# A two-layer decoder trunk on one core: the middle projection by seven half products, and the last four weight sums by accumulating DMAs

## The chip, the core and the metric

The kernel is one program on one NeuronCore of a Trainium2 chip. TensorE (PE) multiplies, VectorE (DVE) and ScalarE (ACT) do elementwise work, GpSimd (POOL) does a little of it and issues software DMAs, SyncE (SP) issues most of the loads. The metric is the device time of one execution, in microseconds (us), lower is better.

## What is computed

Two layers on `x` of 512 tokens by 2048 features, all in float32:

```python
# layer 0
h = rmsnorm(x, e_norm_pre)
p = h @ e_w_in                      # 2048 x 7168, seven column groups
u = concat(ya * silu(a_z), yb * silu(b_z))   # gated convolutions, feature by feature
x = x + rmsnorm(u @ e_w_out, e_norm_post)    # the middle projection, 2048 x 2048
# layer 1
h = rmsnorm(x, o_norm_pre)
v, z = split(h @ o_w_in, 2)                  # 2048 x 4096
g = grouped_linear(pool_means(v) - v, o_c_w) + o_c_b
x = x + rmsnorm((g * o_c_scale * silu(z)) @ o_w_out, o_norm_post)  # the last projection
```

## The kernel before

**Products.** PE has no full float32 product at its full rate here: each operand is split into a rounded part (`w_hi`, `h_hi`, made by ACT) and the rest (`w_lo`, `h_lo`, made by DVE), and each product is three matmuls (lines 602, 604, 606), hi by hi, lo by hi, hi by lo. A matmul streams 512 columns (256 in a few stages). Weights come in slabs of 1 MB (128 partitions by 2048 elements) into `raw` or another buffer; ACT writes slot s mod 4 of `w_hi` once PE is done with slab s - 4 (`slab_done`), DVE then writes `w_lo` (`lo_ready`), and PE waits for `lo_ready`.

**Stages on PE, in order.** `h @ e_w_in` (56 slabs of 48 matmuls), the middle projection (16 slabs of 48, tokens on the output's partitions: `token_major` for three column blocks, `token_major_last` for the fourth, which finishes the tokens tile by tile), `h @ o_w_in` (32 slabs of 48; the first four slabs in two halves of 256 tokens each, h = 0 first), the grouped linear map (four groups of 48), and the last projection.

**The last projection** multiplies two matrices of 2 by 2 blocks (1024 by 1024 of the weights) with seven block products instead of eight. That takes 28 slabs of 24 matmuls. Slabs 0 to 3 are A11, 4 to 7 A12, 8 to 11 N1 and so on; slabs 24 to 27 are the last product, run in four parts: (tokens 0, column block 0), (0, 1), (1, 0), (1, 1), each 24 matmuls. Before the parts (0, 1) and (1, 1) PE waits for `c22(1)` on DVE (line 1638), since that reads the bank that they go on accumulating into; before (0, 0) and (1, 0) for `c22(0)`. Some products take combined weights: T1 (slabs 8 to 11), T2 (12, 13, 16, 17), T3 (20 to 23), T4 (24 to 27), each made from two pieces of 1 MB. Pieces live in the buffers c0 to c3 and b0 to b4. T1 and T3 are added by accumulating DMAs, SBUF to SBUF, issued by POOL (line 564); T2 and T4 by DVE (line 1609). T4's slab 24 is c0 += b1, 25 is c1 += b2, 26 is c2 += b3, 27 is c3 += b4, where b1 to b4 are loaded a fourth time, b1 after T3's last sum has landed (it was that sum's source), b4 after slab 22's low part.

**Norms between the layers.** In the middle, tokens are normed tile by tile (four tiles of 128) under the last column block: squares on ACT (`y_squares`), gain and residual on DVE (`y_gained`, `added`), squares again (`squares`), scaling (`scaled`), then 16 transposes on PE (line 635), rounding on ACT (`h_rounded`, line 915) and the rest on DVE (`h_rest`, line 1314). All these orders are written out by hand, engine by engine; an engine takes its instructions strictly in the order written, so a wait holds all that stands behind it.

## Time and profile before

| | us |
|---|---|
| median of 3 runs | 1384.14 (1383.84 to 1384.17) |
| the profiled execution's own time | 1384.06 |
| its span, first to last instruction | 1382.2 |
| PE busy | 1356.9, 98% of the span |
| DVE / ACT / POOL busy | 765.1 / 415.7 / 112.8 |
| middle projection on PE | 644.9 to 824.4 |
| last projection on PE | 1221.9 to 1374.4 |

"Busy" of PE is the union of its matmuls; the column "idle before" in the lists of groups tells what an engine waited for. A line number is one of the kernel before unless the text says otherwise. Times in windows and timelines count from the span's start.

### The profile page before, as it was taken

What the parts mean: (1) busy time and instruction counts of PE and PEld (TensorE: products, weight loads), DVE (VectorE), ACT (ScalarE), POOL (GpSimd) and SP (SyncE); (2) the same over time, 40 slices, a digit from 0 to 9 for tenths busy, and PEclk for the clock granted to TensorE, in tenths of its full rate; (3) what the DMA queues carried; (4) which work ended last, traced back from release to release, by engine and by line L of the source; (5) the groups of instructions that cost most, each with busy time, mean ns of one, the idle gap of its engine ahead of it and who ended that gap; (6) DMA issues with size and microseconds to landing.
All of it is one profiled execution on the core that took longest, in us unless ns stands there. A gap on an engine that the chain in (4) does not pass through costs nothing.

```text
span 1382.2 us, 15947 instructions
## 1 busy us (share of the span) xinstructions
PE 1356.9 (98%) x6370; PEld 1139.2 (82%) x6370; DVE 765.1 (55%) x784; ACT 415.7 (30%) x430; POOL 112.8 (8%) x109
## 2 busy tenths in 40 slices
PE   5999999999999999999999999999999999999997
PEld 4988888888888888888888889888888888878886
DVE  7588888888763322335322375544532222487778
ACT  5331233232222211224212243222222222345542
POOL 5100000000006400000000000000000001320000
PEclk9999999999999999999999999999999999999999
DMA  8233434343343333331622344433343333279666
GB/s 248 62 97 93 115 91 122 91 121 91 91 121 92 91 92 99 96 111 52 253 91 93 120 152 140 136 91 94 97 112 91 91 93 114 101 225 289 153 217 239
DMA packets 214119, 171.65 MB, mean 124 GB/s; under 512 B 2880, under 2 KB 187328, under 8 KB 211136
## 3 DMA queue, kind: packets, MB, share of 16 engines
q1 hardware_dynamic: 212064, 156.42, 37.1%
q0 software_dynamic: 1152, 8.39, 3.1%
q10 hardware_dynamic: 864, 6.29, 1.2%
q8 instruction: 28, 0.46, 0.1%
q14 instruction: 11, 0.09, 0.0%
HBM read 154.32 MB, written 8.39 MB: 118 GB/s over the span
## 4 chain that ended last, share of the span: by engine, by line
PE 97%; DVE 2%; DMA 0%; issue 0%; ACT 0%; SPq 0%; DVEq 0%; ACTq 0%
PE bank L602 32%; PE bank L604 32%; PE bank L606 32%; DVE h_lo L1349 1%; PE bank L635 1%; DMA rows<-x_t 0%; DVE rows L1342 0%; DVE scratch L1355 0%; DVE diagonals L1320 0%; DVE w_lo L1364 0%; DVE rows L1651 0%; PE bank L664 0%; PE bank L673 0%; ACT scratch L924 0%; SPq L321 0%
## 5 line engine op out<-in xcount | busy, mean ns | idle before, releaser
L602 PE MATMUL bank<-h_hi,w_hi 128*128 128x512 f32 (+1 forms) x1600 | 597.9, 374 | 5.1 <-DVE h_lo L1349 3.9
L604 PE MATMUL bank<-h_lo,w_hi 128*128 128x512 f32 (+1 forms) x1600 | 595.7, 372 | 0.0
L606 PE MATMUL bank<-h_hi,w_lo 128*128 128x512 f32 (+1 forms) x1600 | 595.7, 372 | 0.0
L602 PEld LDWEIGHTS bank<-h_hi,w_hi 128*128 128x128 f32 x1600 | 301.8, 189 | 59.6 <-issue 5.0
L604 PEld LDWEIGHTS bank<-h_lo,w_hi 128*128 128x128 f32 x1600 | 301.9, 189 | 52.8 <-issue 0.5
L606 PEld LDWEIGHTS bank<-h_hi,w_lo 128*128 128x128 f32 x1600 | 301.8, 189 | 52.3
L1287 DVE TENSOR_TENSOR w_lo<-raw,w_hi 128x2048 fp32r<-128x2048 f32 x105 | 243.6, 2320 | 123.7 <-ACT w_hi L892 108.9
L892 ACT ACTIVATE w_hi<-raw 128x2048 fp32r<-128x2048 f32 x106 | 202.7, 1912 | 152.7 <-PE bank L606 117.1
L1382 DVE SCALAR_TENSOR_TENSOR rows<-shifted,vecs,rows 128x512 f32 x256 | 198.0, 776 | 42.2 <-ACT rows L962 10.9
L602 PE MATMUL bank<-w_hi,h_hi 128*128 128x512 f32 x480 | 187.0, 390 | 0.0
L606 PE MATMUL bank<-w_hi,h_lo 128*128 128x512 f32 x480 | 186.8, 389 | 0.0
L604 PE MATMUL bank<-w_lo,h_hi 128*128 128x512 f32 x480 | 186.8, 389 | 0.0
L602 PEld LDWEIGHTS bank<-w_hi,h_hi 128*128 128x128 f32 x480 | 90.1, 188 | 19.1
L606 PEld LDWEIGHTS bank<-w_hi,h_lo 128*128 128x128 f32 x480 | 90.1, 188 | 18.9
L604 PEld LDWEIGHTS bank<-w_lo,h_hi 128*128 128x128 f32 x480 | 90.1, 188 | 18.2
L1548 DVE TENSOR_TENSOR shifted<-shifted 128x512 f32<-128x512 f32 x40 | 27.7, 693 | 84.7 <-ACT shifted L1082 83.9
L1567 DVE TENSOR_SCALAR scratch<-scratch,vecs x16 | 7.8, 488 | 109.9 <-ACT scratch L1103 109.9
L559 POOL TENSOR_TENSOR h_lo<-rows,h_hi 128x512 fp32r<-128x512 f32 x16 | 24.9, 1590 | 356.0 <-ACT h_hi L1091 356.0
L1103 ACT ACTIVATE scratch<-bank 128x512 f32 (+1 forms) x16 | 9.6, 598 | 133.0 <-PE bank L606 133.0
L980 ACT ACTIVATE scratch<-bank 128x512 f32<-128x512 f32 x16 | 9.6, 598 | 131.2 <-PE bank L606 131.2
L1082 ACT ACTIVATE shifted<-bank 128x512 f32<-128x512 f32 x16 | 9.6, 598 | 122.1 <-PE bank L606 122.1
L971 ACT ACTIVATE rows<-shifted,vecs 128x512 f32 x8 | 5.8, 724 | 125.0 <-DVE shifted L1407 125.0
(115 smaller groups left out, 629.5 us busy)
## 6 DMA issues: line engine op xcount, KB each, us to landing
raw<-e_in SPq DMA_DIRECT2D x54, 1024.0 KB, 5.6
raw<-o_in SPq DMA_DIRECT2D x32, 1024.0 KB, 6.2
raw<-e_out SPq DMA_DIRECT2D x16, 1024.0 KB, 5.0
spare<-o_out SPq DMA_DIRECT2D x12, 1024.0 KB, 8.9
scratch<-o_out SPq DMA_DIRECT2D x10, 1024.0 KB, 6.8
rows<-x_t SPq DMA_DIRECT2D x8, 512.0 KB, 6.6
x_mid<-rows ACTq DMA_DIRECT2D x4, 1024.0 KB, 4.8
raw<-o_cw SPq DMA_DIRECT2D x4, 1024.0 KB, 5.4
```

The costliest lines, as they stand in the source:

```text
L559: nc.gpsimd.tensor_tensor(h_lo[:, k, :], rows[:, k, :], f32(h_hi[:, k, :]), ALU.subtract).then_inc(pool_lo_ready, 1)
L602: nc.tensor.matmul(dst, w[0], m[0], start=first, stop=False, skip_group_check=goes_on)
L604: nc.tensor.matmul(dst, w[0], m[1], start=False, stop=False, skip_group_check=goes_on)
L606: return nc.tensor.matmul(dst, w[1], m[0], start=False, stop=last, skip_group_check=goes_on)
L635: last = nc.tensor.transpose(bank[4 + j][:, i * P:(i + 1) * P], row[:, k * P:(k + 1) * P], ident[:, :])
L892: nc.scalar.activation(w_hi[:, slot, :], raw[:, slot % RAW, :], ACT.Copy)\
L980: nc.scalar.activation(sz[buf], bank[q][:, :], ACT.Silu)\
L1082: nc.scalar.activation(v_row[:, PAD:], bank[q][:, :], ACT.Copy)\
L1287: nc.vector.tensor_tensor(w_lo[:, slot, :], raw[:, slot % RAW, :], f32(w_hi[:, slot, :]), ALU.subtract)\
L1349: nc.vector.tensor_tensor(h_lo[at], rows[at], f32(h_hi[at]), ALU.subtract)\
L1382: ins = nc.vector.scalar_tensor_tensor(out=dst, in0=row[:, at:at + T], scalar=tap(name, c, width, j), in1=dst, op0=ALU.mult, op1=ALU.add)
L1548: link(nc.vector.tensor_tensor(dst[:, PAD:], src[:, PAD:], src[:, PAD - step:PAD - step + T], ALU.add))
```

## The change

The middle projection now runs as the last one does: seven half products, 28 slabs of 24 matmuls (672 where 768 stood), with the same list of loads, sums, squares and block additions (`projection(0)`; the last is `projection(1)`). In both, T4 is no longer added by DVE but by four more accumulating DMAs (`t4_added`), so twelve of the sixteen weight sums are DMAs: four more in the last projection, twelve new ones in the middle.

The norm of the first two token tiles of the middle moves under that projection's last product (slabs 24 to 27): DVE takes mean squares, gains, `mid_added` (times the reciprocal root, plus the residual row; two instructions of 1024 columns) and `mid_scaled` (the second norm) between its low parts and `c22`. The post gain goes to buffer b1 once T4's first sum has landed; the residual rows of x to b0 and b4, the third and fourth to c3 and b0; SP issues these behind the fourth load of b4. PE transposes tile 0 after part (0, 1), tile 1 after part (1, 0), tile 2 after the first half slab of `h @ o_w_in` and tile 3 after the third. The high part of that stage's first slab (`split_ahead(AT_O1 - 1, 1)`) stands on ACT behind `mid_squares(2)`, its low part on DVE behind `mid_added(2)`.

`h` for `o_w_in` is stored with the two token halves apart, so a moving operand of 512 tokens is two runs of 256 (`both_halves`). In `rows` the blocks lie in chunks of 256, which makes several reads and writes on ACT, DVE and in stores three-dimensional. `group(g)` no longer waits for `pool_lo_ready`.

```diff
-E2 = NBLK
+E2 = 7
...
-SLOT_A, SLOT_B, SLOT_C, SLOT_D = range(4)
+SLOT_AT = ({"A": 2, "B": 1, "C": 3, "D": 0}, {"A": 0, "B": 1, "C": 2, "D": 3})
...
-        ADDED_AT = {n: i + 1 for i, n in enumerate((12, 13, 16, 17, 24, 25, 26, 27))}
+        FIRST = (AT_E2 * SLOTS, AT_O2 * SLOTS)
+        LOADS = {name: (1 if name[0] == "c" else 4) for name in buffers[0]}
+        ADDED_AT = {n: i + 1 for i, n in enumerate((12, 13, 16, 17))}
...
+            def sums_loads(layer, w):
+
+                low_done(layer, 4)
...
+                sp.wait_ge(t3_added[3], 16 * (layer + 1))
+                low_done(layer, 19)
+                piece(layer, w, "b1", 1, 0, 0, 0)
+                low_done(layer, 20)
+                piece(layer, w, "b2", 1, 0, 0, 1)
+                low_done(layer, 21)
+                piece(layer, w, "b3", 1, 0, 1, 0)
+                low_done(layer, 22)
+                piece(layer, w, "b4", 1, 0, 1, 1)
+
...
+            sums_loads(0, e_out)
+            sp.wait_ge(t4_added[0], 16)
+            sp.dma_start(gain_post[0], e_post.to_broadcast([P, D])).then_inc(gain_loaded, 16)
+            low_done(0, 23)
+            sp.dma_start(x_resid[0], x[0:P, :]).then_inc(resid_loaded[0], 16)
+            sp.wait_ge(t4_added[3], 16)
+            sp.dma_start(x_resid[1], x[P:2 * P, :]).then_inc(resid_loaded[1], 16)
+            low_done(0, 26)
+            sp.dma_start(gain_next, o_pre.to_broadcast([P, D])).then_inc(gain_next_loaded, 16)
+            low_done(0, 27)
+            sp.dma_start(x_resid[2], x[2 * P:3 * P, :]).then_inc(resid_loaded[2], 16)
             with sp.Fori(0, O1V + O1Z) as g:
...
+            sums_loads(1, o_out)
+            low_done(1, 24)
+            sp.dma_start(gain_post[1], o_post.to_broadcast([P, D])).then_inc(gain_loaded, 16)
...
+            def add_by_dma(layer, dst, src, dst_loads, src_loads, news):
+
+                for name, count in ((dst, dst_loads), (src, src_loads)):
+                    pool.wait_ge(piece_loaded[name], 16 * (count + layer * LOADS[name]))
+                nc.gpsimd.dma_start(buffers[layer][dst], buffers[layer][src],
+                                    accum_op=ALU.add).then_inc(news, 16)
...
+                add_by_dma(layer, "b0", "b1", 4, 3, t3_added[3])
+                pool.wait_ge(lo_ready, first + 13)
+                add_by_dma(layer, "c0", "b1", 1, 4, t4_added[0])
+                pool.wait_ge(lo_ready, first + 14)
+                add_by_dma(layer, "c1", "b2", 1, 4, t4_added[1])
+                pool.wait_ge(lo_ready, first + 17)
+                add_by_dma(layer, "c2", "b3", 1, 4, t4_added[2])
+                pool.wait_ge(lo_ready, first + 18)
+                add_by_dma(layer, "c3", "b4", 1, 4, t4_added[3])
+
+            weight_sums(0)
             powers(MID, 2 * TT)
+            pool.wait_ge(normed, 2 * TT)
+            nc.gpsimd.memset(shifted[:, :, 0:PAD], 0.0).then_inc(pads_set, 1)
 
...
+            def both_halves(k):
+                return h_halves[0][:, :, k, :], h_halves[1][:, :, k, :]
...
+                        between(tt, nb)
+
+            def first_transposes(tt, nb):
+                if (tt, nb) == (0, 1):
+                    transposes(0, x_resid[0])
+                elif (tt, nb) == (1, 0):
+                    transposes(1, x_resid[1])
...
+            def o_half_slab(q, h):
...
+                    m = h_halves[0][:, h, k, :], h_halves[1][:, h, k, :]
+                    last = product(bank[q][:, h * HALF:(h + 1) * HALF], weights(q, k, P), m,
+                                   k == 0, k == KT - 1)
...
+            projection(0, AT_E2 + 1, lambda b: uses4(b, "mid") + 1, first_transposes)
...
+                    o_half_slab(q, h)
+                    if h == 0 and q in (0, 2):
+                        transposes(2 + q // 2, x_resid[2 + q // 2])
...
+            high_dma(0, 25, t4_added[1])
+            high_dma(0, 26, t4_added[2])
+            c_squares(0, C22, 0, c22_ready, 8)
+            high_dma(0, 27, t4_added[3])
+            mid_squares(0)
+            c_squares(0, C22, 1, c22_ready, 10)
+            mid_squares(1)
+            h_rounded(0)
+            last_squares(0, 0)
+            h_rounded(1)
+            act.dma_start(x_resid[3], x[3 * P:4 * P, :]).then_inc(resid_loaded[3], 16)
+            mid_squares(2)
+            split_ahead(AT_O1 - 1, 1, STEPS)
+            last_squares(0, 1)
+            split_ahead(AT_O1 - 1, 2, STEPS)
+            mid_squares(3)
+            h_rounded(2)
+            split_ahead(AT_O1 - 1, 3, STEPS)
+            split_ahead(AT_O1, 0, STEPS)
+            h_rounded(3)
 
...
+            dve.wait_ge(c_squared, 8)
+            mean_square(MID)
+            dve.wait_ge(gain_loaded, 16)
+            gain(0, c_half(C11, 0), c_half(C11, 0), 0, 8)
+            gain(0, c_half(C12, 0), c_half(C12, 0), NH, 8)
+            low(0, 25)
+            c22(0, 0)
+            dve.wait_ge(c_gained, 2)
+            mid_added(0)
+            low(0, 26)
+            mean_square(MID + 2)
+            gain(0, c_half(C11, 1), c_half(C11, 1), 0, 8)
+            gain(0, c_half(C12, 1), c_half(C12, 1), NH, 8)
+            low(0, 27)
+            c22(0, 1)
...
+            mid_mean(0)
+            dve.wait_ge(c_gained, 4)
+            mid_added(1)
+            mid_scaled(0)
+            for tt in range(2):
+                gain(0, c_half(C22, tt), c_half(C22, tt), NH, 12)
+            mid_mean(1)
+            mid_scaled(1)
             h_rest(0)
-            mid_norm(2)
+            dve.wait_ge(c_squared, 14)
+            mean_square(MID + 4)
+            last_gain(0, 0, 0)
+            last_gain(0, 1, 0)
+            for nb in range(2):
+                dve.wait_ge(bank_free[2 * nb], AT_O1 + 1)
+            dve.wait_ge(c_gained, 6)
             h_rest(1)
-            split_ahead(end, 1)
-
-            def under_last_norm():
-                h_rest(2)
-                split_ahead(end, 2)
-
-            mid_norm(3, under_last_norm, lambda: split_ahead(end, 3))
-            split_ahead(end + 1, 0)
+            mid_added(2)
+            split_ahead(AT_O1 - 1, 1)
+            mid_mean(2)
+            last_gain(0, 0, 1)
+            dve.wait_ge(c_squared, 16)
+            mean_square(MID + 6)
+            last_gain(0, 1, 1)
+            for nb in range(2):
+                dve.wait_ge(bank_free[2 * nb + 1], AT_O1 + 1)
+            mid_scaled(2)
+            mid_added(3)
+            split_ahead(AT_O1 - 1, 2)
+            h_rest(2)
+            mid_mean(3)
+            split_ahead(AT_O1 - 1, 3)
+            mid_scaled(3)
+            split_ahead(AT_O1, 0)
             h_rest(3)
...
+            projection(1)
+            low(1, 25)
+            c22(1, 0)
+            low(1, 26)
+            dve.wait_ge(c_squared, 16 + 8)```

POOL's DMAs of the last projection, kernel before, from T1's last sum on (`spare2`, `spare3`, `spare4` are b2, b3, b4; `raw` is c0 and c1; `scratch` the others):

```order
L564 DMA scratch_55<-spare2_70 128x2048
L564 DMA spare2_70<-spare3_71 128x2048
L564 DMA spare3_71<-spare4_72 128x2048
L564 DMA spare4_72<-scratch_55 128x2048
L564 DMA scratch_55<-scratch_55 128x2048
L530 TENSOR_TENSOR rstd_67<-meansq_66,minus_half_62 128x1 x4
```

The same place in the kernel after:

```order
L582 DMA spare4_74<-scratch_55 128x2048
L582 DMA scratch_55<-scratch_55 128x2048
L582 DMA raw_52<-scratch_55 128x2048
L582 DMA raw_52<-spare2_1_71 128x2048
L582 DMA scratch_55<-spare3_1_73 128x2048
L582 DMA scratch_55<-spare4_74 128x2048
L553 TENSOR_TENSOR rstd_67<-meansq_66,minus_half_62 128x1 x4
```

Four DMAs, the sums for slabs 24 to 27, now stand behind the four of T3 in POOL's queue.

DVE at the end of the last projection, kernel before (L1609 is a sum, L1601 a low part, L1638 `c22`):

```order
L1609 TENSOR_TENSOR raw_52<-raw_52,spare2_70 128x2048
L1601 TENSOR_TENSOR w_lo_54<-raw_52,w_hi_53 128x2048
L1609 TENSOR_TENSOR scratch_55<-scratch_55,spare3_71 128x2048
L1601 TENSOR_TENSOR w_lo_54<-raw_52,w_hi_53 128x2048
L1638 TENSOR_TENSOR rows_51<-rows_51,bank0 128x512
L1638 TENSOR_TENSOR rows_51<-rows_51,bank1 128x512
L1609 TENSOR_TENSOR scratch_55<-scratch_55,spare4_72 128x2048
L1601 TENSOR_TENSOR w_lo_54<-scratch_55,w_hi_53 128x2048
```

DVE at the end of the middle projection, kernel after (L1454 is a low part, L1521 a gain, L1513 `c22`, L1592 `mid_added`):

```order
L1454 TENSOR_TENSOR w_lo_54<-raw_52,w_hi_53 128x2048
L1291 TENSOR_REDUCE total_65<-sumsq_64 128x1
L1292 TENSOR_SCALAR meansq_66<-total_65 128x1
L1521 TENSOR_TENSOR rows_51<-rows_51,scratch_55 128x4x256 x2
L1454 TENSOR_TENSOR w_lo_54<-raw_52,w_hi_53 128x2048
L1513 TENSOR_TENSOR rows_51<-rows_51,bank0 128x2x256
L1513 TENSOR_TENSOR rows_51<-rows_51,bank1 128x2x256
L1592 SCALAR_TENSOR_TENSOR rows_51<-rows_51,rstd_67,scratch_55 128x4x256 x2
L1454 TENSOR_TENSOR w_lo_54<-scratch_55,w_hi_53 128x2048
```

Where sums stood, the norm of the first tokens stands, ahead of the low parts of slabs 25, 26 and 27.

ACT in the middle, kernel after, from the rounding of tile 1 (L920) to the high part of the first slab of `o_w_in` (L907); L1171 is `mid_squares`, L1190 the load of the fourth residual row:

```order
L920 ACTIVATE h_hi_49<-bank7 128x4x128
L1190 DMA scratch_55<-x 128x2048
L1171 ACTIVATE junk_63,sumsq_64<-rows_51 128x512 x2
L1176 DMA x_mid<-rows_51 128x4x256
L1171 ACTIVATE junk_63,sumsq_64<-rows_51 128x512 x2
L1176 DMA x_mid<-rows_51 128x4x256
L907 ACTIVATE w_hi_53<-raw_52 128x2048
```

In the kernel before, that high part stood here, ahead of the squares of a third tile:

```order
L915 ACTIVATE h_hi_49<-bank7 128x4x128
L1056 DMA scratch_55<-x 128x2048
L892 ACTIVATE w_hi_53<-raw_52 128x2048
L1028 ACTIVATE shifted_56,sumsq_64<-bank3 128x512
L915 ACTIVATE h_hi_49<-bank4 128x4x128
```

The squares of tile 2 (four instructions) moved ahead of the high part.

## Rows read from the trace of the kernel before

**Rows 1.** The page: the span, shares of the engines, the chain that ended last.

```profile
span 1382.2 us, 15947 instructions
...
PE 1356.9 (98%) x6370; PEld 1139.2 (82%) x6370; DVE 765.1 (55%) x784; ACT 415.7 (30%) x430; POOL 112.8 (8%) x109
...
PE 97%; DVE 2%; DMA 0%; issue 0%; ACT 0%; SPq 0%; DVEq 0%; ACTq 0%
```

**Rows 2.** PE in stretches: from:to, length, busy time (matmuls), clock, DMA share, GB/s.

```profile
80.00:420.00 340.00, 340.00 (x1501) 1.00 0.37 102
...
670.00:790.00 120.00, 120.00 (x531) 1.00 0.31 106
...
1215.00:1370.00 155.00, 155.00 (x686) 1.00 0.75 231
```

**Rows 3.** DVE's timeline, end of the last projection: start, duration, instruction, [idle before].

```profile
1330.59 2.29 DVE L1609 TENSOR_TENSOR raw<-raw,scratch 128x2048 f32<-128x2048 f32 x1 [0.85 <-DMA scratch<-o_out]
...
1354.65 2.29 DVE L1601 TENSOR_TENSOR w_lo<-scratch,w_hi 128x2048 fp32r<-128x2048 f32 x1 [2.48 <-ACT w_hi L1128]
1356.86 1.28 DVE L1638 TENSOR_TENSOR rows<-rows,bank 128x512 f32<-128x512 f32 x2
```

**Rows 4.** ACT's timeline, same place: slab 27's high part, and the last square.

```profile
1352.70 1.92 ACT L1128 ACTIVATE w_hi<-scratch 128x2048 fp32r<-128x2048 f32 x1 [2.30 <-PE bank L606]
...
1374.40 0.60 ACT L1162 ACTIVATE junk<-bank 128x512 bf16<-128x512 f32 x1 [4.75 <-PE bank L606]
```

**Rows 5.** SP's timeline: the fourth loads of b1, then of b2, b3, b4.

```profile
1325.50 0.37 SPq L394 DMA_DIRECT2D scratch<-o_out  x1
1325.92 4.22 SPq L394 DMA_DIRECT2D spare<-o_out  x3
```

**Rows 6.** DMA queues in 1328:1337, loads alone: packets, MB, share of 16 engines.

```profile
q1 hardware_dynamic: 1780, 3.55, 105.2%
```

**Rows 7.** The same view in 1320:1324, one accumulating DMA alone.

```profile
q0 software_dynamic: 107, 0.88, 108.0%
```

**Rows 8.** The same view in 1257:1266, accumulating DMAs (q0) and loads (q1) together.

```profile
q0 software_dynamic: 219, 1.66, 88.7%
q1 hardware_dynamic: 218, 0.45, 14.7%
```

**Rows 9.** Issue to landing: the accumulating DMAs of line 564, then `spare`'s in 1240:1350.

```profile
DMA to landing us min/median/max: 7.0/7.7/14.9
...
DMA to landing us min/median/max: 5.0/8.0/21.6
```

**Rows 10.** Groups with shapes, 1205:1382: count, busy us, mean ns, idle before.

```profile
L1162 ACT ACTIVATE junk<-rows 128x512 bf16<-128x512 f32 x12 | 7.4, 615 | 3.0 <-DVE rows L1638 3.0
L1644 DVE TENSOR_TENSOR rows<-rows,raw 128x1024 f32<-128x1024 f32 x6 | 7.1, 1220 | 0.0
...
L1651 DVE SCALAR_TENSOR_TENSOR rows<-rows,rstd,scratch 128x1024 f32<-128x1024 f32 x4 | 5.0, 1282 | 0.1
```

**Rows 11.** DVE's and ACT's timelines in the middle: rest, rounding and first high part.

```profile
819.28 2.47 DVE L1314 TENSOR_TENSOR h_lo<-bank,h_hi 128x512 fp32r<-128x512 f32 x4
821.67 2.28 DVE L1287 TENSOR_TENSOR w_lo<-raw,w_hi 128x2048 fp32r<-128x2048 f32 x1
...
815.49 2.04 ACT L915 ACTIVATE h_hi<-bank 128x512 fp32r<-128x512 f32 x4
817.39 1.94 ACT L892 ACTIVATE w_hi<-raw 128x2048 fp32r<-128x2048 f32 x1
```

**Rows 12.** PE's timeline after its start: 256-column matmuls, two early, two later.

```profile
22.60 0.41 PE L606 MATMUL bank<-h_hi,w_lo 128*128 128x256 f32 x1
22.81 0.41 PE L602 MATMUL bank<-h_hi,w_hi 128*128 128x256 f32 x1
...
25.28 0.28 PE L602 MATMUL bank<-h_hi,w_hi 128*128 128x256 f32 x1
25.40 0.28 PE L604 MATMUL bank<-h_lo,w_hi 128*128 128x256 f32 x1
```

More of the change, by code:

```diff
@@ new lines, in _, with mid_added @@
+            low(0, 3)
+            a_low(0, "B", 0, quarter(A12), FORMS[0]["a12"][0])
+            projection(0)
+            def mid_added(t):
+                n = MID + 2 * t
+                dve.wait_ge(rstd_ready, NORM_ORDER.index(n) + 1)
+                dve.wait_ge(resid_loaded[t], 16)
+                for m, c in enumerate((C11, C12) if t < 2 else (C21, C22)):
+                    at = c_half(c, t % 2)
+                    nc.vector.scalar_tensor_tensor(
+                        out=at, in0=at, scalar=rstd[:, n:n + 1],
+                        in1=chunks(x_resid[t][:, m * NH:(m + 1) * NH]),
+                        op0=ALU.mult, op1=ALU.add).then_inc(x_mid_ready, 1)
```

1116 lines of the change are left out of this document (505 added, 611 removed).

## The prediction

> **What bounds the kernel.** I read the page first, then PE by stretches, then the other engines and the DMA queues where the change works. The page says that PE is busy for 98% of the span and that the chain that ended last runs 97% on PE [rows 1]. The stretches say that this is no average over mixed stages: in long windows of `h @ e_w_in`, of the middle projection and of the last one PE is busy all the time, with a matmul of 512 columns each 0.2265, 0.2260 and 0.2260 us (340 / 1501, 120 / 531, 155 / 686) [rows 2]. So each matmul taken away is worth 0.2265 us, as long as nothing else comes late, and each microsecond that another engine or a DMA comes late is paid in full. The question is thus what is ready only just in time.
>
> I call E the start of slab 24 in the last projection. PE is done at 1374.4 [rows 4], the last product is 96 matmuls or 21.8 us, so E is 1352.6; ACT's high part of slab 27, which waits for slab 23 alone, starts at 1352.70 and confirms it [rows 4]. A part takes 24 x 0.2265 = 5.4 us, so part (0, 1) wants the first `c22(1)` at E + 5.4 = 1358.1. DVE's low part of slab 27 starts at 1354.65 and `c22(1)` behind it at 1356.86, its first half done some 0.7 later [rows 3]: 1357.5, half a microsecond before PE wants it. This place has no slack.
>
> **Removed.** The middle projection falls from 768 to 672 matmuls: 96 x 0.2265 = 21.7 us less. The 64 transposes stay. The products lie on the path now, so this is a gain in full.
>
> **T4 by DMA in the last projection.** Off DVE go four sums of 2.3 us, but the one for slab 24 already waited 0.85 us for its piece b1 [rows 3], so the pieces come just in time now; what is new comes on top. The loads: b1 is issued at 1325.50, b2 to b4 up to 1330.1 [rows 5]. What does a transfer cost? Loads alone move 3.55 MB in 9 us with all 16 engines busy [rows 6], so a piece of 1.05 MB takes 2.66 us of all engines; one alone lands 5.0 us after its issue [rows 9], 2.3 more than it moves. An accumulating DMA alone moves 0.88 MB in 4 us with the engines likewise busy [rows 7], 4.8 us each; it lands after 7.0 at best [rows 9], 2.2 more. Nothing overlaps, the engines being full, so the last sum lands no sooner than 1325.5 + 2.3 + 4 x 2.66 + 4 x 4.8 = 1357.6. Both kinds together: q0 takes 88.7% of the engines' time and the loads 14.7% [rows 8]. So the load of b4, in the ring behind b2 and b3, is starved while the first three sums move (loads in that stage took up to 21.6 us [rows 9]); the fourth sum, which needs b4, starts only then, and its own 2.2 us come on top: 1359.8. The gain row and a residual row of 1 MB each share the engines with it, up to 2 x 2.66; I take 4 of those 5.3 and have 1363.8, E + 11.2.
>
> From there the high part takes 1.9 [rows 4], the low part 2.3 and half of `c22(1)` 0.7 [rows 3]: 1368.7, where PE wants it at 1358.1. **10.5 us** of PE standing still. The bounds: with the fourth sum at 1357.6, 4.3 us; with 14.9 us for it (the longest [rows 9]) from a landing of b4 at 1352, 13.6.
>
> **The same in the middle.** The list of slabs, loads and sums is the same and DVE is not behind there, so the last sum lands at about E0 + 9 to E0 + 11 (E0, its slab 24). By that alone the wait is 8 to 10 us. But a second chain runs on DVE. The gain e_post may be loaded only into b1, once the first sum has landed (about E0 - 12: 1325.5 + 5.0 for b1, then 10 to 12 for a sum among loads), and stands in SP's ring behind the starved b4: I take it to land at E0 + 3. The first gain stands ahead of the low part of slab 25 on DVE, and all that follows is queued: gains 2 x 1.2, low part 2.2, `c22(0)` 1.2, `mid_added` 2 x 1.25, low part 2.2, mean square 0.3, gains 2.4, low part 2.2, half of `c22(1)` 0.6 [rows 3, 10]: 16.0. So `c22(1)` is ready at E0 + 19 where PE wants it at E0 + 5.4: 13.6; I take **12**, since b1's chain may be some 2 us ahead here. Lower bound 4 (no gain row late, last sum as early as above), upper 15.
>
> **The norm at the start of `h @ o_w_in`.** Let Z be the end of tile 1's transposes. PE has 5.4 us of part (1, 1) left. Meanwhile, each waiting for the one before: rounding of tile 1, of which the first quarter is 0.6 [rows 11], `h_rest(1)` 2.5 [rows 11], `mid_added(2)` 2.5 [rows 10], the second pair of squares 1.3 [rows 10], the high part of the first slab 1.9 and its low part 2.3 [rows 11]. That is 11.1, so PE stands for 5.7. Then DVE has mean squares and gains (1.8), `mid_scaled(2)` and `mid_added(3)` (2 x 2.5) and the second slab's low part 2.2: Z + 20, where PE, with the half slab (5.4) and tile 2's transposes (1.7), is at Z + 18.3. Together **7.4**. In the kernel before that high part stood ahead of the squares and was done at 819.3 where PE wanted it at 824.4 [rows 11].
>
> **TensorE's clock.** PE waits long in three or four places then. Just after its idle start the 256-column matmuls come 0.21 us apart, the lower level of 1.2 GHz; later 0.12, the upper of 2.4 [rows 12]. About ten matmuls at 0.09 us more are 1 us. I add **2** for the ramps that are not under another wait (0 to 4). The Trainium skill, "TensorE: Matmul & The Clock Gate", Part 1, says that the clock falls back on idleness, so it speaks for a ramp after each long wait; this trace has no long gap behind its start to show it. [...]
>
> **At nothing.** Reads in chunks of 256 on ACT and DVE: `h_rest` writes such chunks and takes 0.62 each [rows 11], like a contiguous block. The start of the middle projection: the form of A11 is made from the second quarter of the last slab of `e_w_in` on, some 3 us ahead of PE. A moving operand in two runs: taken at nothing, since no row has one. Its bound is that each run costs like an instruction of its own: 0.12 us for 256 columns [rows 12] twice is 0.24 against 0.2265, times 28 x 48 matmuls, 18 us. One square at a time on ACT: under 1 us, under PE's products. The Trainium skill, "DMA: Bandwidth & Descriptors", Queues, rings and completion order, has each engine take a packet from each ring in turn; if that gave the loads half of the time, b4 and the gain would be there some 10 us sooner, and the middle's term would be near 9 instead of 12. The split of 88.7 to 14.7 [rows 8] says otherwise.
>
> **The sum.** 1384.1 - 21.7 + 10.5 + 12 + 7.4 + 2 = **1394.3**, against the profiled execution's own 1384.06, which is within 0.1 of the median, so I forecast 1394.
>
> **The rivals.**
> - Faster (1): the sums come in time, as T1's and T3's do now, and DVE, rid of four sums, is early. Speaks for it: no row of before shows PE waiting for a DMA. Against: T3's sums come one by one between loads, and T4's four come within 25 us. Then only the 7.4 remains: 1369.7. It decides at the landing of the last sum: before E + 1 all is hidden.
> - In between (2): both projections at their lower bounds, 4.3 and 4, or halfway to mine: 1378 to 1387.
> - Slower still (3): two runs cost, up to 18 more; or each wait brings a full ramp. 1397 to 1412.
> - That the products are not fewer can be excluded: the order shows 28 slabs of 24 in the middle.
>
> **How the numbers follow.** Mine 0.60 (1388 to 1401), (1) 0.15, (2) 0.15, of it a third below 1381.3, half within 0.2% of before and a sixth above that, (3) 0.10. A measurement can tell about 0.2%, 2.8 us. Faster 0.15 + 0.05 = 0.20, same 0.08, slower 0.72. The range leaves out (1) and the far part of (3): 1379 to 1402.
>
> **What would show it.** In the profile after: the middle projection has 672 matmuls; PE idle some 10 us before part (0, 1) in the last projection, released by DVE `c22(1)`, with ACT's high part of slab 27 released by a DMA; in the middle the same with DVE waiting for the gain row, and a wait of 6 us before the first half slab of `h @ o_w_in`. If high part 27 in both is released by PE, the step on the DMAs is wrong. If matmuls of `o_w_in` come further apart than 0.2265, two runs cost.

## The result: slower by 1.2%

| kernel | median us | runs | lowest to highest |
|---|---|---|---|
| before | 1383.99 | 4 | 1383.78 to 1384.17 |
| after | 1399.97 | 4 | 1398.93 to 1403.02 |

The ratio is 1.012, 95% interval 1.0106 to 1.0133. The forecast was 1394 with a range of 1379 to 1402 and 0.72 for slower. The profiled execution took 1398.93 us, the shortest of its four, 14.9 more than that of before (1384.06).

### The profile page after: what moved, and what is told of

It reads as the page before. It is cut to its first block, busy times and chain, and to the rows that moved or that the text cites. A ratio compares the mean times of both kernels' runs of the same rounds, so it can differ in the third digit from the quotient of the medians.

```text
span 1397.1 us, 15727 instructions
## 1 busy us (share of the span) xinstructions
PE 1342.1 (96%) x6274; PEld 1125.4 (81%) x6274; DVE 810.0 (58%) x781; ACT 450.7 (32%) x445; POOL 128.0 (9%) x126
## 4 chain that ended last, share of the span: by engine, by line
PE 90%; DMA 5%; DVE 4%; ACT 1%; issue 1%; DVEq 0%; ACTq 0%; POOLq 0%
PE bank L630 30%; PE bank L632 30%; PE bank L634 30%; DMA spare<-o_out 2%; DMA scratch<-e_post 1%; DMA raw<-scratch 1%; DMA scratch<-spare 1%; DVE h_lo L1336 1%; DVE w_lo L1454 1%; DVE scratch L1342 1%; ACT w_hi L1013 0%; PE bank L666 0%; DVE rows L1329 0%; DMA rows<-x_t 0%; DVE rows L1592 0%
## 5 line engine op out<-in xcount | busy, mean ns | idle before, releaser
L630 PE MATMUL bank<-h_hi,w_hi 128*128 128x512 f32 (+1 forms) x1600 | 598.5, 374 | 10.7 <-DVE w_lo L1281 4.9
L632 PE MATMUL bank<-h_lo,w_hi 128*128 128x512 f32 (+1 forms) x1600 | 596.2, 373 | 0.0
L634 PE MATMUL bank<-h_hi,w_lo 128*128 128x512 f32 (+1 forms) x1600 | 596.1, 373 | 0.0
L630 PEld LDWEIGHTS bank<-h_hi,w_hi 128*128 128x128 f32 x1600 | 302.3, 189 | 65.9 <-issue 5.7
L632 PEld LDWEIGHTS bank<-h_lo,w_hi 128*128 128x128 f32 x1600 | 302.3, 189 | 52.6 <-issue 0.5
L634 PEld LDWEIGHTS bank<-h_hi,w_lo 128*128 128x128 f32 x1600 | 302.3, 189 | 52.3
L1281 DVE TENSOR_TENSOR w_lo<-raw,w_hi 128x2048 fp32r<-128x2048 f32 x89 | 207.1, 2327 | 53.5 <-ACT w_hi L907 46.6
L630 PE MATMUL bank<-w_hi,h_hi 128*128 128x512 f32 x448 | 177.2, 395 | 24.1 <-DVE rows L1513 24.0
L907 ACT ACTIVATE w_hi<-raw 128x2048 fp32r<-128x2048 f32 x90 | 171.9, 1910 | 77.6 <-PE bank L634 64.9
L632 PE MATMUL bank<-w_lo,h_hi 128*128 128x512 f32 x448 | 176.0, 393 | 0.0
L634 PE MATMUL bank<-w_hi,h_lo 128*128 128x512 f32 x448 | 175.8, 392 | 0.0
L630 PEld LDWEIGHTS bank<-w_hi,h_hi 128*128 128x128 f32 x448 | 85.2, 190 | 43.4 <-DVE rows L1513 25.8
L634 PEld LDWEIGHTS bank<-w_hi,h_lo 128*128 128x128 f32 x448 | 85.2, 190 | 18.1
L632 PEld LDWEIGHTS bank<-w_lo,h_hi 128*128 128x128 f32 x448 | 85.4, 191 | 17.6
L1454 DVE TENSOR_TENSOR w_lo<-scratch,w_hi 128x2048 fp32r<-128x2048 f32 x26 | 59.9, 2303 | 52.7 <-ACT w_hi L1013 52.7
L1013 ACT ACTIVATE w_hi<-scratch 128x2048 fp32r<-128x2048 f32 x26 | 49.8, 1916 | 70.2 <-DMA scratch<-spare 22.7
L1454 DVE TENSOR_TENSOR w_lo<-raw,w_hi 128x2048 fp32r<-128x2048 f32 x16 | 37.4, 2336 | 41.4 <-ACT w_hi L1013 41.4
```

The lines of the kernel that those rows point to most:

```text
L630: nc.tensor.matmul(dst, w[0], m[0], start=first, stop=False, skip_group_check=goes_on)
L632: nc.tensor.matmul(dst, w[0], m[1], start=False, stop=False, skip_group_check=goes_on)
L634: return nc.tensor.matmul(dst, w[1], m[0], start=False, stop=last, skip_group_check=goes_on)
L907: nc.scalar.activation(w_hi[:, slot, :], raw[:, slot % RAW, :], ACT.Copy)\
L1013: nc.scalar.activation(w_hi[:, s % SLOTS, :], buffers[layer][SPLIT_FROM[s]], ACT.Copy).then_inc(hi_ready, 1)
L1281: nc.vector.tensor_tensor(w_lo[:, slot, :], raw[:, slot % RAW, :], f32(w_hi[:, slot, :]), ALU.subtract)\
```

## The profile after

The page says where to look: PE has fewer matmuls (6274 for 6370, [rows 1]) and is busy for 96% of a longer span. The chain that ended last, 97% on PE before, has 9% on DMAs and DVE. The last row is the group of the high by high matmuls in the two projections; what stands behind the bar is the idle time before them.

```profile
span 1397.1 us, 15727 instructions
...
PE 1342.1 (96%) x6274; PEld 1125.4 (81%) x6274; DVE 810.0 (58%) x781; ACT 450.7 (32%) x445; POOL 128.0 (9%) x126
...
PE 90%; DMA 5%; DVE 4%; ACT 1%; issue 1%; DVEq 0%; ACTq 0%; POOLq 0%
...
L630 PE MATMUL bank<-w_hi,h_hi 128*128 128x512 f32 x448 | 177.2, 395 | 24.1 <-DVE rows L1513 24.0
```

Line 1513 is `c22`. The timeline of PE at the waits (start, duration, instruction, idle before): three are released by `c22`, one by a low part.

```profile
775.09 0.39 PE L634 MATMUL bank<-w_hi,h_lo 128*128 128x512 f32 x1
783.92 0.80 PE L630 MATMUL bank<-w_hi,h_hi 128*128 128x512 f32 x1 [8.44 <-DVE rows L1513]
...
790.82 0.39 PE L634 MATMUL bank<-w_hi,h_lo 128*128 128x512 f32 x1
794.44 0.79 PE L630 MATMUL bank<-w_hi,h_hi 128*128 128x512 f32 x1 [3.23 <-DVE rows L1513]
...
815.65 0.39 PE L634 MATMUL bank<-w_hi,h_lo 128*128 128x512 f32 x1
820.98 0.58 PE L630 MATMUL bank<-h_hi,w_hi 128*128 128x256 f32 x1 [4.93 <-DVE w_lo L1281]
...
1358.13 0.39 PE L634 MATMUL bank<-w_hi,h_lo 128*128 128x512 f32 x1
1370.86 0.79 PE L630 MATMUL bank<-w_hi,h_hi 128*128 128x512 f32 x1 [12.35 <-DVE rows L1513]
1371.45 0.63 PE L632 MATMUL bank<-w_lo,h_hi 128*128 128x512 f32 x1
...
1374.41 0.39 PE L634 MATMUL bank<-w_hi,h_lo 128*128 128x512 f32 x1
```

The last four show both parts of a loss. From the end of the matmul at 1358.13 (0.23 later by the spacing) to 1370.86 PE stands for 12.5 us. Then eight matmuls take 3.55 us (1374.41 - 1370.86) where eight take 1.81 at 0.2265: 1.7 us at TensorE's lower level, 0.427 us for 512 columns. I call this a ramp.

By PE's timeline the middle, from its first product to the end of tile 3's transposes, took 198.5 us before (644.94 to 843.46) and 198.7 after (644.76 to 843.43). The last projection, first to last matmul, took 152.1 before (1221.88 to 1373.97) and 166.8 after (1221.89 to 1388.71). So **the middle lost just what its 96 matmuls gave, and the last projection lost 14.7 us with nothing in return.**

Why was `c22` late? The chain of waits for the last projection, followed back from its end (start, duration, what):

```profile
1329.78 24.80 DMA spare<-o_out
1354.65 0.60 issue
1355.25 10.70 DMA scratch<-spare
1365.97 1.92 ACT w_hi L1013
1368.16 1.96 issue
1370.12 0.69 DVE rows L1513
```

The load of b4 took 24.8 us from issue to landing, the fourth sum behind it 10.7 more, then come high part, low part (the second "issue" covers it) and `c22(1)`. While b4 was under way the engines worked almost wholly for the sums (queues in 1336:1341, as in [rows 8]: packets, MB, share of 16 engines):

```profile
q0 software_dynamic: 117, 0.96, 91.9%
q1 hardware_dynamic: 115, 0.24, 14.0%
```

The same for the middle's wait before part (0, 1). This chain does not go through the last sum, but through the gain row and DVE's queue behind it: 753.08 is T4's first sum, whose landing lets the gain row be loaded.

```profile
753.08 11.59 DMA raw<-scratch
764.70 13.99 DMA scratch<-e_post
779.85 1.22 DVE rows L1521
784.47 2.39 DVE rows L1592 x2
786.86 2.20 DVE w_lo L1454
791.59 2.20 DVE w_lo L1454
793.79 0.61 DVE rows L1513
```

And a stretch of `h @ o_w_in`, for the moving operand in two runs (the columns of [rows 2]). In the same stretch of before PE has the same 1325 matmul records in 300 us.

```profile
900.00:1200.00 300.00, 300.00 (x1325) 248.43 (x1324) 103.01 (x109) 72.86 (x67) 14.97 (x11) 1.00 0.35 102
```

## The experiments

**First group: who adds T4.** `BY_DVE` lists, for each layer, the slabs whose sum DVE makes; `add_t4` adds on DVE if the slab is in it and does nothing otherwise, POOL leaves these out, and `high_t4` waits on ACT for the one or the other. The edit (here the last projection; from kernel to kernel the list differs, and where DVE makes sums of the middle too, `add_t4(0, 27)` stands ahead of `mid_added(0)`):

```diff
+        BY_DVE = ((), (24, 25, 26, 27))
...
-                high_dma(layer, 24, t4_added[0])
+                high_t4(layer, 24)
...
                 low(layer, 22)
+                add_t4(layer, 24)
                 low(layer, 23)
                 c12(layer, 1)
+                add_t4(layer, 25)
                 low(layer, 24)
+                add_t4(layer, 26)
...
             c22(1, 0)
+            add_t4(1, 27)
```

*The last projection by DVE (e1_last_dve).*

> The changed kernel, but T4's four weight sums of the last projection are added by DVE again, at the places they had in the kernel before; the middle is as changed. Theory (the accumulating DMAs of the last projection cost what its trace shows: 12.5 us of PE standing before part (0, 1), 1.7 us of matmuls at the lower clock behind that wait, 0.4 us at the start of slab 24, 14.7 together against before): the wait goes altogether, 1399.97 - 14.7 = 1385.3 us, and the last projection takes 152.1 us as in the kernel before. Rival (the chunked reads and the third dimension slow DVE and ACT, so that DVE can't carry its four sums in time any more): 2 to 5 us of wait remain, 1387 to 1390. Rival (the DMA sums only moved a wait that is there anyway): no change, 1400.

Measured 1385.14 us (1384.13 to 1385.80, ratio to before 0.9998 to 1.0017): the theory's figure. The last projection takes 152.1 us again, and no wait of it is left; b4, issued at 1329.9, lands after 11.8 us, not 24.8 (the view of its line):

```profile
DMA to landing us min/median/max: 11.8/11.8/11.8
```

This rules out both rivals: chunked reads don't keep DVE from its sums, and the wait isn't there without the DMA sums.

*The middle by DVE (e2_mid_dve).*

> The changed kernel, but T4's four sums of the middle projection are added by DVE, at the same places as in the last projection of the kernel before; the gain row is loaded once DVE has added slab 24's sum. The last projection is as changed. In the changed kernel PE stood for 8.6 and 3.4 us in the middle and paid 1.6 us of slow clock behind each, 15.2 us. Theory (DVE is then the bound, since two pairs of gains, mid_added and a mean square, 7.5 us, stand ahead of c22(1), which came 0.5 us early without them): a wait of about 7.0 us and one ramp of 1.7 remain, 1399.97 - 15.2 + 8.7 = 1393.5 us. Rival (the late DMAs alone were the cause): all 15.2 us go, 1384.8. Rival (DVE's order was the cause, and four more sums of 2.3 us make it worse): 1400 or more.

Measured 1391.19 us (1390.81 to 1392.41). The middle took 188.3 us in place of 198.7, so 10.4 less, where I had expected 6.5: the wait before (0, 0) went, the one before (0, 1) fell to 3.2 us and not to 7.0. DVE is the bound, as the theory says, but it had more room ahead of the last product than I gave it.

```profile
784.26 0.80 PE L645 MATMUL bank<-w_hi,h_hi 128*128 128x512 f32 x1 [3.04 <-DVE rows L1541]
```

The time fell by less than 10.4 since this execution's last projection, which is the changed one, took 169.1 us, not 166.8: in the four kernels that leave it as changed (after, this one, e5_mid_order and e6_o_order) it took 166.8 to 169.1 us. The 2.3 us more here are a wait before part (0, 1) that ended 1.3 us later, counted from the projection's first matmul, and a ramp behind it that cost 2.8 us in place of 1.7.

*Both by DVE (e3_both_dve).*

> The changed kernel with T4's sums by DVE in both projections. Theory: the two savings add up, -14.7 and -6.5, 1378.8 us, which would be 5 us faster than the kernel before. If the waits were one common cost (the queues of both projections held by the same thing) they would not add up.

Measured 1374.42 us (1374.26 to 1376.11), ratio to before 0.9933, interval 0.9917 to 0.9950: **faster than both kernels.** The two savings of the trace, 10.4 and 14.7, add up: 1398.9 - 25.1 = 1373.8 against a profiled execution of 1374.38.

*Only the fourth sum by DVE (e4_one_dve).*

> The changed kernel, but in the last projection the fourth sum of T4 alone (slab 27, from b4) is added by DVE; the first three stay DMAs. Theory (the load of b4, starved beside three sums, lands at 1354.6 as it did, and only the fourth sum behind it goes, 11 us of DMA for 2.3 us of DVE): c22(1) half done at 1362.4 where it was at 1370.8, so PE still stands for about 4 us and pays its ramp; 1391.6 us. Rival (the cost is the engine time of the sums, a quarter each): -3.7 us, 1396.3. Rival (everything hangs on the last sum alone, and b4 comes in time without it): -14.7, 1385.3.

Measured 1394.13 us (1392.71 to 1395.61): 5.8 less by the medians, between the theory (8.4 less) and a quarter each (3.7 less). By the trace the last projection took 162.2 us for 166.8, 4.6 less, which is nearer to the quarter. b4 took 26.5 us to land, as starved as before, but the chain of waits now goes through the third sum, which landed at 1358.3, so that slab 26 was late as well:

```profile
1346.30 11.98 DMA scratch<-spare
```

And b4's load, from the view of its line:

```profile
DMA to landing us min/median/max: 26.5/26.5/26.5
```

So the fourth sum alone is not the cause. It is the row of them, with loads beside them that get about a seventh of the engines.

*The first two by DMA, the last two by DVE, in both projections (e8_split).*

> The changed kernel with T4's first two sums (slabs 24, 25) by DMA and its last two (26, 27) by DVE, in both projections. With all four by DVE the middle still had a wait of 3.2 us and its ramp of 1.6 before part (0, 1), DVE being the bound. Theory (the first two sums land at 764.7 and 770.3, ahead of need, and take 4.6 us off DVE; b4 is starved only until the second has landed, some 3 us ahead of the last product): that wait goes too, 1374.4 - 4.8 = 1369.6 us. Rival (two sums among the loads already make b3, b4 or the gain row late): 1376 to 1386.

Measured 1389.88 us (1388.99 to 1390.09): the rival. In the last projection two sums still cost 5.4 us (157.5 for 152.1). In the middle the gain row is late again, since it waits for the first sum and shares the engines with the second; it lands at 774.3 where with four sums by DVE it landed at 764.0. DVE then works without a pause for 18 us until `c22(1)`, and the middle takes 198.5 us, as if nothing had been undone.

```profile
774.34 2.36 DVE L1549 TENSOR_TENSOR rows<-rows,scratch 128x1024 f32<-128x1024 f32 x2 [3.41 <-DMA scratch<-e_post]
...
791.53 1.28 DVE L1541 TENSOR_TENSOR rows<-rows,bank 128x512 f32<-128x512 f32 x2
```

*T4 by DMA alone, in the kernel before (f1_before_t4).*

```diff
+            for n, (s, dst, src) in enumerate(((13, "c0", "b1"), (14, "c1", "b2"),
+                                               (17, "c2", "b3"), (18, "c3", "b4"))):
+                pool.wait_ge(lo_ready, LAST + s)
...
+                add_by_dma(dst, src, t4_added[n])
...
-            add(24, 4)
```

> The kernel before with one part of the change alone: T4's four sums in the last projection by accumulating DMAs in place of DVE. Theory (this part costs by itself what the changed kernel lost there, 12.5 us of wait, 1.7 of slow clock behind it and 0.4 at the start of slab 24): 1384.0 + 14.7 = 1398.7 us. Rival (the loss needs something else of the change, the chunked layout or the state the middle leaves the queues in): 1384 to 1390.

Measured 1399.81 us (1399.26 to 1400.50), 15.6 more than before beside it (1384.26), where I had expected 14.7; by its trace the last projection took 167.2 us for 152.1, 15.1 more. The same part costs about the same in a kernel that has nothing else of the change:

```profile
1371.09 0.79 PE L610 MATMUL bank<-w_hi,h_hi 128*128 128x512 f32 x1 [11.31 <-DVE rows L1651]
```

**Second group: which chain binds the middle (e5_mid_order).** DVE takes two low parts and `c22(0)` ahead of the gains:

```diff
+            low(0, 25)
+            c22(0, 0)
+            low(0, 26)
             dve.wait_ge(gain_loaded, 16)
             gain(0, c_half(C11, 0), c_half(C11, 0), 0, 8)
             gain(0, c_half(C12, 0), c_half(C12, 0), NH, 8)
-            low(0, 25)
-            c22(0, 0)
             dve.wait_ge(c_gained, 2)
             mid_added(0)
-            low(0, 26)
```

> The changed kernel, but in the middle DVE takes the low parts of slabs 25 and 26 and c22(0) ahead of the first two gains (and so ahead of the wait for the gain row). T4's sums stay DMAs. Theory (two chains end at c22(1): DVE's queue from the gain row's landing at 778.7 on, and the last sum's landing at 785.98; with the queue eased the last sum is next): high part, low part and half of c22(1) behind 785.98 give 790.8 where part (0, 1) began at 794.4, so 3.6 us less, and one wait of 10 us in place of two, so one ramp of 1.6 less: 1394.8 us. Rival (the gain row alone made the middle late): 15.2 us go, 1384.8. Rival (the last sum alone set it, DVE's order is nothing): no change but the place of the wait, 1398 to 1400.

Measured 1399.14 us (1398.00 to 1400.06). The time alone can't be told from the changed kernel's and lies where the second rival put it, 1398 to 1400. The trace decides: the mechanism is right and the sum is not. Part (0, 1) began at 791.26 (790.8 expected), 3.2 sooner, and the last sum is what binds now:

```profile
786.37 1.91 ACT L1013 ACTIVATE w_hi<-scratch 128x2048 fp32r<-128x2048 f32 x1 [6.77 <-DMA scratch<-spare]
...
791.26 0.79 PE L630 MATMUL bank<-w_hi,h_hi 128*128 128x512 f32 x1 [10.16 <-DVE rows L1513]
```

But I had counted the first wait's ramp as a gain of its own. It had lain inside the time until 794.4 already, since `c22(1)` ends at its own time whatever PE does. And the one ramp left was longer, 12 matmuls at 0.427 in place of 6 or 7, 2.7 us in place of 1.5. The middle gave 1.6 us, not 5.2.

**The order at the start of `h @ o_w_in` (e6_o_order).**

```diff
-            mid_squares(2)
             split_ahead(AT_O1 - 1, 1, STEPS)
+            mid_squares(2)
...
-            mid_added(2)
             split_ahead(AT_O1 - 1, 1)
+            mid_added(2)
```

> The changed kernel, but the first slab of h @ o_w_in is split ahead of tile 2's norm: on ACT its high part stands before mid_squares(2), on DVE its low part before mid_added(2). Theory (the 5.1 us and the ramp of 1.7 before the first half slab come from this order alone): they go, and tile 2's own chain, 2.2 us later on DVE, makes PE wait some 1.3 us before tile 2's transposes: 1394.5 us. Rival (the wait only moves to tile 2's transposes, since the whole chain of the norm is the bound): 1398 or more. Rival (nothing behind it is late): 1393.2.

Measured 1401.99 us (1401.27 to 1403.78): my theory fell, the first rival held. The stage began without a wait, 6.7 us sooner (5.1 are the wait; the rest is that the wait before (0, 1), 2.1 us this time, had no ramp behind it), and PE waited behind it, for tile 2's transposes and again before the second half slab, with a ramp of 2.8 us there; tile 3's transposes came 0.6 us later than in the changed kernel. (The rest of the difference is this execution's last projection, 168.4 us.)

```profile
822.44 2.70 PE L666 MATMUL bank<-ident,scratch 128*128 128x128 f32 x16 [1.99 <-DVE scratch L1603]
828.23 0.58 PE L630 MATMUL bank<-h_hi,w_hi 128*128 128x256 f32 x1 [3.09 <-DVE w_lo L1281]
```

**What a ramp costs (e7_warm).** Ahead of three waits, matmuls of no use:

```diff
+            WARM = {(0, 0, 0): 34, (0, 0, 1): 12, (1, 0, 1): 50}
...
+                        stay_warm(layer, WARM.get((layer, tt, nb), 0))
                         pe.wait_ge(c22_ready, at + 2 * nb + tt + 1)
```

> The changed kernel with matmuls that compute nothing wanted (into bank 4, free at that time, 512 columns each) put on PE ahead of the waits of the last product: 34 and 12 in the middle, before parts (0, 0) and (0, 1), and 50 in the last projection before part (0, 1); at 0.2265 us they fill 7.7 of 8.6, 2.7 of 3.4 and 11.3 of 12.5 us of waiting. Theory (the seven matmuls at 0.427 us behind each wait are the lower clock, which comes from the idleness, and cost 1.5 to 1.7 us each): they go, 1399.97 - 4.9 = 1395.1 us, and the matmuls behind the waits come 0.2265 apart at once. Rival (those seven are slow for another reason, such as fresh weights or DMA traffic): no change, 1400.

Measured 1397.95 us (1397.11 to 1399.45). All three ramps are gone (the second matmul behind each wait starts 0.33 or 0.34 us after the first and the rest come 0.23 apart, where it was 0.59 and 0.43), so it is the idle time that brings them:

```profile
784.64 0.50 PE L630 MATMUL bank<-w_hi,h_hi 128*128 128x512 f32 x1 [1.22 <-DVE rows L1523]
784.97 0.39 PE L632 MATMUL bank<-w_lo,h_hi 128*128 128x512 f32 x1
...
795.15 0.50 PE L630 MATMUL bank<-w_hi,h_hi 128*128 128x512 f32 x1 [2.06 <-DVE rows L1523]
...
1370.93 0.50 PE L630 MATMUL bank<-w_hi,h_hi 128*128 128x512 f32 x1
1371.26 0.40 PE L632 MATMUL bank<-w_lo,h_hi 128*128 128x512 f32 x1
```

But the time fell by 2.0 us (1.6 between the profiled executions), not 4.9: the middle took 198.6 us, as in the changed kernel. A ramp ahead of another wait is free, because that wait ends when DVE ends. Only the last projection's, with nothing but products behind it, gave its 1.7 (165.1 us for 166.8).

**Third group: on from T4 by DVE in both.** In f2_best DVE takes tile 1's mean square and gains behind `c22(1)`:

```diff
             low(0, 26)
-            mean_square(MID + 2)
-            gain(0, c_half(C11, 1), c_half(C11, 1), 0, 8)
-            gain(0, c_half(C12, 1), c_half(C12, 1), NH, 8)
             low(0, 27)
             c22(0, 1)
+            mean_square(MID + 2)
+            gain(0, c_half(C11, 1), c_half(C11, 1), 0, 8)
+            gain(0, c_half(C12, 1), c_half(C12, 1), NH, 8)
             mid_mean(0)
+            mid_scaled(0)
             dve.wait_ge(c_gained, 4)
             mid_added(1)
-            mid_scaled(0)
```

> T4 by DVE in both projections (1374.42 us), and in the middle DVE takes the mean square and the two gains of tile 1 behind c22(1), and mid_scaled(0) ahead of mid_added(1). With T4 by DVE the middle's part (0, 1) began at 784.8 where PE wanted it at 781.5, DVE having worked without a pause since 759. Theory (DVE's queue is the bound of that wait, 2.7 us of it are moved behind): c22(1) half done at 782, the wait and its ramp go; tile 0's transposes then wait for mid_scaled(0), which waits for the gain row o_pre (landed 787.0): first half at 788.2, 3.3 us sooner than 791.8: 1371.1 us. Rival (the time is set by tile 1's norm, later now by mid_scaled(0) ahead of it): 1374 or more. Rival (everything behind comes in time): 1369.5.

Measured 1375.59 us (1373.78 to 1376.09), the first rival, and not to be told from the 1374.42 of e3_both_dve (1374.26 to 1376.11). The wait before (0, 1) fell to 0.5 us and had no ramp, tile 0's transposes start at 787.3, and tile 1's wait: DVE scales tile 1 at 793.71, and with T4 by DVE and the old order it did so at 793.57. DVE has the same work in any order. PE is released a little later by DVE's `h_rest(0)` (line 1324), which must free the bank and stands behind that:

```profile
793.71 2.48 DVE L1634 SCALAR_TENSOR_TENSOR spare<-rows,rstd,scratch 128x1024 f32<-128x1024 f32 x2 [0.66 <-POOL rstd L564]
...
796.94 1.30 PE L681 MATMUL bank<-ident,spare 128*128 128x128 f32 x5 [2.19 <-DVE h_lo L1324]
```

Then f3_best, the same with 20 matmuls of no use before `h @ o_w_in`, and one swap on DVE:

```diff
-            mid_added(3)
             split_ahead(AT_O1 - 1, 2)
+            mid_added(3)
```

> As f2_best, and before h @ o_w_in 20 matmuls that compute nothing wanted (4.5 us of the 5.1 that PE waits there), and DVE splits the second slab of that stage ahead of mid_added(3). The first half slab ran at 0.213 us for 256 columns for its first 17 matmuls, 1.7 us more than at 0.117. Theory (the ramp goes; the second slab's low part, now at 2.4 us less, is ready as PE asks for it; tile 3's scaling, 2.3 us later, is about in time): 1.5 us less than f2_best. Rival (as in the middle of e7_warm, where two of three ramps removed moved nothing because the next wait ends at a fixed time): the same as f2_best within 0.5 us.

Measured 1378.64 us (1377.96 to 1380.14): neither. Both edits are in this one kernel, so only the trace tells them apart. The ramp, 2.7 us in f2_best, went (tile 2's transposes came at 816.6, not 819.6), but the swap I had added to make use of it cost more. `mid_added(3)` later means that ACT's squares of tile 3, and behind them its rounding of tile 2, are later; DVE waits 2.4 us for that, and PE for the low part behind:

```profile
821.98 2.48 DVE L1333 TENSOR_TENSOR h_lo<-bank,h_hi 128x512 fp32r<-128x512 f32 x4 [2.40 <-ACT h_hi L944]
...
827.59 0.58 PE L645 MATMUL bank<-h_hi,w_hi 128*128 128x256 f32 x1 [3.37 <-DVE w_lo L1313]
```

Last, g1_pool_gains: T4 by DVE in both, and four gains on POOL:

```diff
+            powers(MID, 1)
+            pool.wait_ge(gain_loaded, 16)
+            pool_gain(c_half(C11, 1), 0, 8)
+            pool_gain(c_half(C12, 1), NH, 8)
+            powers(MID + 1, 2)
+            for tt in range(2):
+                pool_gain(c_half(C22, tt), NH, 12)
...
-            for tt in range(2):
-                gain(0, c_half(C22, tt), c_half(C22, tt), NH, 12)
```

> T4 by DVE in both projections (1374.42 us), and in the middle the two gains of tile 1 and the two of C22 are taken by POOL, which is idle there, in place of DVE: 4.7 us less for DVE, about 12 us (four blocks of 1024 at 3.04 us, from its 1.52 us for 128x512) for POOL. In f2_best the order on DVE was changed and tile 1's scaled row was done at 796.1 as before. Theory (DVE's whole queue from 759 to 796 is the bound of the middle now, whatever its order): c22(1) comes 2.3 us sooner, tile 1's scaling some 4.7 sooner, and PE, which then waits at tile 0's transposes for the gain row o_pre (787.0, first half scaled 788.2), begins tile 1's at 795.5 instead of 799.0: 1374.4 - 3.4 = 1371.0 us. Rival (POOL and DVE slow each other when both work, or POOL's powers come late behind its gains): 1374 or more.

Measured 1379.35 us (1378.44 to 1380.15), the rival. DVE's groups with shapes in the stretch 786:796 (count, busy us, mean ns), first of e3_both_dve, then of this kernel with POOL's in 766:796.

```profile
L1623 DVE SCALAR_TENSOR_TENSOR rows<-rows,rstd,spare 128x1024 f32<-128x1024 f32 x2 | 2.5, 1282 | 0.0
```

```profile
L1637 DVE SCALAR_TENSOR_TENSOR rows<-rows,rstd,spare 128x1024 f32<-128x1024 f32 x2 | 4.6, 2349 | 0.3 <-issue 0.3
L1648 DVE SCALAR_TENSOR_TENSOR scratch<-rows,rstd,scratch 128x1024 f32<-128x1024 f32 x2 | 4.6, 2334 | 0.0
...
L629 POOL TENSOR_TENSOR rows<-rows,scratch 128x1024 f32<-128x1024 f32 x4 | 13.8, 3460 | 0.2 <-ACT junk L1106 0.2
```

DVE's 1.28 us became 2.3 beside POOL's work, and POOL's gains took 3.46, where I had estimated 3.04 from twice its 1.52 for 128x512. What DVE was rid of (4.7 us) it more than paid back: these two pairs took 9.2 us for 5.0, and a low part and T4's last sum beside the other gains 7.8 for 4.6, about 7.5 us more in all. That agrees with the Trainium skill, "SBUF — State Buffer", Who interferes with whom, which says that a DVE instruction with two SBUF inputs contends with a GpSimd instruction that reads SBUF.

## Why the prediction held, point by point

The forecast was 6 us too low. Its mechanisms held: the starved load and the late last sum, DVE's queue behind the gain row, and the norm's chain before `h @ o_w_in`. Its sizes did not: three costs were too low by 2.4, 1.7 and 3.0 us and one too high by 2.3, so that a part of the error cancelled by luck. What the changes cost was forecast as 31.9 us (10.5 + 12 + 7.4 + 2); measured it is 14.9 + 21.7 = 36.6, and the other 1 us is the median above the profiled execution.

| term | forecast | measured in the trace of after |
|---|---|---|
| 96 matmuls fewer | -21.7 | -21.7 |
| last projection, T4 by DMA | 10.5 | 12.5, and 0.4 at slab 24's start |
| middle, until part (0, 1) | 12 | 13.7 |
| start of `h @ o_w_in` | 7.4 | 5.1 |
| ramps not under another wait | 2 | 1.5 + 1.8 + 1.7 = 5.0 |

- **The last projection: right in kind, 2 us short.** b4 landed at 1354.65 and the fourth sum at 1365.95, where I had 1363.8. The sum itself took 10.7 us, 3.7 more than the 7.0 of one alone, which is about the 4 that I allowed for loads beside it. What came late is its start: 1355.25, where my sum implies 1352.8 (1359.8 less 7.0). I had counted the gain row and one residual row, both beside the last sum. There were two residual rows, and in 1325.5:1354.65, before b4 had landed, the loads moved 4.87 MB, 0.7 more than the four pieces. In 1354.65:1366, beside the sum, they moved 2.47 MB more (the view of the queues):

```profile
q1 hardware_dynamic: 348, 2.47, 51.8%
```

That makes 3.1 MB of rows, three and not two. No run holds these rows back, so what they cost by themselves is not shown. e1_last_dve and f1_before_t4 price this part at 14.8 and 15.6, ramp included, and the landing times of b4, 11.8 against 24.8, show the starved load.
- **The middle: the chain held to 0.1 us, the discount did not.** The gain row landed at 778.69, 3.4 after E0 = 775.3 (forecast 3); part (0, 1) began at E0 + 19.1 (forecast 19). The chain gave 13.7; I took 12, "since b1's chain may be some 2 us ahead", and it was not. The place was partly wrong: I had all of the wait before part (0, 1), but 8.6 of it stood before (0, 0), since the low part of slab 25 stands behind the gains. e5_mid_order shows that two chains end there 3 us apart, and that the gain row's is the longer.
- **The start of `h @ o_w_in`: 5.1 for the 5.7 forecast, and the second wait of 1.7 did not come.** The first half slab took 7.5 us (820.98 to 828.51): 48 matmuls at 0.12 are 5.8, where I had written 5.4, and the ramp's 1.8 came on top, so the second slab's low part, done at 829.8, was ready when tile 2's transposes were through. e6_o_order shows how close it is: with the first wait taken away, the second appears.
- **The clock: the term that was mis-sized, by 3 us.** I took 2 of a possible 4 from ten matmuls; four ramps came, each 1.5 to 1.8, one of them hidden. The three others came to 5.0 us, above the 4 that I had as the most: no row of before has a ramp behind a wait, and the runs price one at 1.4 to 3.0 us. The Trainium skill, "TensorE: Matmul & The Clock Gate", Part 1, says that the clock falls back on idleness; the traces agree, since e7_warm, which fills the idle time, has none of the three ramps.
- **At nothing:** two runs of 256 columns cost nothing (1325 matmul records in 300 us before and after), which takes rival (3)'s first half away; its second half, a full ramp for each wait, is what happened. 1399.97 lies in that rival's span (1397 to 1412) and in my own case's (1388 to 1401). The chunked reads cost nothing that e1_last_dve could show: its last projection took the 152.1 us of before.
- **The queue rule.** I set the share of [rows 8] against the Trainium skill, "DMA: Bandwidth & Descriptors", Queues, rings and completion order, as if its turns meant equal time. They mean equal packets: 117 to 115 above, 219 to 218 in [rows 8]. By those rows an accumulating DMA's packet is 8.2 KB (0.96 MB by 117) and a load's 2.1 KB, and it takes the engines 6.5 times as long (91.9 by 117 against 14.0 by 115), so a load that gets every second packet gets about a seventh of the time. Rule and row agree; my reading of the rule was wrong, my number was not.
- **Rival (1),** all sums in time, fell with the rows of after. It had argued from T3's sums; those come one by one (in after those of the last projection were issued at 1277.7, 1293.5, 1305.9 and 1318.4), and PE waited for none of them in any run.

Left open: why the last projection's loss varied between 14.7 and 17.0 us with the same code there. What varied is when the wait before part (0, 1) ended, 149.0 us behind the projection's first matmul in after and 149.8 to 150.3 in e5_mid_order, e6_o_order and e2_mid_dve, and the ramp behind it, 1.7 to 2.8 us; waits of 1.8 to 2.8 us before slab 24, which came in those three and not in after, lie inside that time. Why a ramp takes 12 slow matmuls in one place and 6 to 8 in another is open too.

## What to carry to other kernels

An accumulating DMA inside SBUF is not free because DVE is spared: 1 MB took 4.8 us of all 16 engines and left the loads beside it about a seventh of them, so count the loads that stand behind it. Sums that come one by one, as T3's do, cost nothing in these runs; four within 25 us ahead of their use did. Fewer matmuls pay only where something else has room: here 21.7 us of products were given back within the same stage, and the version that keeps 9.6 of them (T4 by DVE in both, 1374.42 us) is 0.7% faster than the kernel before. When you add up waits of one engine, add only up to the last one that ends at a time of its own: a ramp or a wait in front of it is already in it.
